# A hybrid decoder trunk: the weights of the attention steps combined a step earlier, and a beginning in quarters

## What is computed

```
proj = rms_norm(h) @ w_in                      # 1024 -> 2048: u (512), q, k, v (512 each)
y_pool = windowed means of u, 2/4/8/16 wide, minus u, times a 128x128 matrix per group
for each of 4 heads:                           # halves of 64 of q and k
    a = softmax(q1 k1^T / 8 + bias) - lam * softmax(q2 k2^T / 8 + bias)
    o = rms_norm(a @ v, subln_w) * 0.8
h = h + concat(y_pool, o) @ w_out
```

## Time and profile before

| what | value |
|---|---|
| time, median of 3 runs | 1526.26 us (1521.80 to 1531.88) |
| the profiled execution's own time | 1525.67 us |
| its span, first to last instruction | 1523.7 us |
| PE busy | 1415.4 us, 93% of the span |
| DVE, ACT, POOL busy | 695.0, 507.1, 395.0 us |
| mean granted clock of PE | 0.981 |

### The profile page before, as it was taken

One profiled execution on the slowest core, in us unless ns is written; L12 is line 12 of the kernel. 1 busy time (PEld: TensorE's weight loads), 2 busy tenths in 40 slices (PEclk: granted clock), 3 DMA queues, 4 the chain that ended last, 5 costly groups with the idle time before them and its releaser, 6 DMA issues.

```text
span 1523.7 us, 28397 instructions
## 1 busy us (share of the span) xinstructions
PE 1415.4 (93%) x11848; PEld 1185.4 (78%) x11848; DVE 695.0 (46%) x962; ACT 507.1 (33%) x723; POOL 395.0 (26%) x490
## 2 busy tenths in 40 slices
PE   6998889999999999898988989889789999999996
PEld 5766478888888888677777877777678888888885
DVE  5445533333333332766567576665533333333222
ACT  5233434232323222424424334244233232323221
POOL 2003412122212011534435343343322122212010
PEclk9998999999999999899999999999999999999999
DMA  7364612423233312002110220120032222233211
GB/s 268 146 197 164 201 54 86 164 83 110 83 120 115 113 67 83 28 29 70 42 56 29 68 72 28 56 68 30 1 136 100 104 89 99 94 120 114 100 53 56
DMA packets 31325, 140.92 MB, mean 92 GB/s; under 512 B 4457, under 2 KB 6761, under 8 KB 18954
## 3 DMA queue, kind: packets, MB, share of 16 engines
q1 hardware_dynamic: 31242, 139.75, 26.4%
HBM read 128.63 MB, written 11.11 MB: 92 GB/s over the span
## 4 chain that ended last, share of the span: by engine, by line
PE 83%; DVE 11%; issue 3%; ACT 2%; DMA 0%; POOL 0%; DVEq 0%; SPq 0%; ACTq 0%; POOLq 0%
PE P L1522 57%; PE P L1881 8%; PE P L1872 7%; DVE arena L1308 2%; PE P L1887 2%; DVE wl L1030 1%; PE P L1849 1%; DVE arena L1349 1%; DVE arena L1452 1%; PE P L2036 1%; PE P L2028 1%; PE P L1935 1%; ACT wh L695 1%; DVE arena L1396 1%; PE P L1722 1%
## 5 line engine op out<-in xcount | busy, mean ns | idle before, releaser
L1522 PE MATMUL P<-zh,wh 128*128 128x260 f16 x1728 | 334.4, 275 | 17.1 <-DVE wl L1030 13.2
L1522 PE MATMUL P<-zl,wh 128*128 128x260 f16 x1728 | 334.2, 275 | 0.0
L1522 PE MATMUL P<-zh,wl 128*128 128x260 f16 x1728 | 333.8, 274 | 0.0
L1522 PE MATMUL P<-arena,wh 128*128 128x260 f16 x1920 | 291.9, 273 | 5.3 <-DVE arena L1160 3.2
L1030 DVE SCALAR_TENSOR_TENSOR wl<-stage,wh 128x2048 f16<-128x2048 f32 (+1 forms) x77 | 189.4, 2460 | 224.5 <-ACT wh L661 196.0
L1522 PEld LDWEIGHTS P<-arena,wh 128*128 128x128 f16 x1920 | 185.6, 97 | 35.5 <-DVE arena L1160 3.3
L1522 PEld LDWEIGHTS P<-zh,wh 128*128 128x128 f16 x1728 | 166.7, 97 | 49.8 <-issue 23.0
L1522 PEld LDWEIGHTS P<-zh,wl 128*128 128x128 f16 x1728 | 168.0, 97 | 27.0
L1522 PEld LDWEIGHTS P<-zl,wh 128*128 128x128 f16 x1728 | 167.9, 97 | 27.0
L1522 PE MATMUL P<-arena,wl 128*128 128x260 f16 x960 | 184.5, 273 | 0.0
L1881 PE MATMUL P<-arena 128*128 128x128 f32 x1152 | 156.1, 288 | 28.8 <-issue 18.2
(11 more groups left out here) (300 smaller groups left out, 1583.6 us busy)
## 6 DMA issues: line engine op xcount, KB each, us to landing
stage<-w_gu SPq DMA_DIRECT2D x44, 1024.0 KB, 4.9
stage<-w_in SPq DMA_DIRECT2D x24, 1024.0 KB, 5.2
stage<-w_dn SPq DMA_DIRECT2D x16, 1408.0 KB, 5.8
arena<-cache_k SPq DMA_DIRECT2D x32, 256.0 KB, 3.5
stage<-w_out SPq DMA_DIRECT2D x8, 1024.0 KB, 6.5
arena<-cache_v SPq DMA_DIRECT2D x32, 256.0 KB, 2.9
arena<-delta_state SPq DMA_DIRECT2D x8, 512.0 KB, 3.6
o_ds<-arena SPq DMA_DIRECT2D x8, 512.0 KB, 6.7
```

The lines of the kernel that those rows point to most:

```text
L1522: mm = nc.tensor.matmul(pm[j][:, c, :], w[:, wslot, o:o + 128], x[:, k, c * CH:(c + 1) * CH], start=(k == first and w is wh and x is xh), ...
```

## The change

Loop, DVE: `combine` runs one step ahead. `combine(0)` stands between the leaving of tiles 4 and 5, and step s does maximum s+1, the leaving of its tile, `combine(s+1)`, and the weight split after that. Loop, PE: scores of step 1 stand ahead of the value transposes, whose copies are awaited only before the first turn; `decode_probs` stands before the turn of step 9, the first value product in step 9; the others stay. ACT copies the decode weights out before the turned ones. The last pooling group's split moves from behind the loop into step 15.

End: the first 12 matmuls of tile 0 of the output projection, then the last head's norm and the decode norm, then the rest of both tiles' pooling groups, then the heads. ACT takes the last head out before it turns to the decode norm.

Beginning: `hT` and the first weight unit arrive in quarters in turn, and ACT, DVE and PE work by quarters; both tiles of unit 0 grow together, and the statistics come after them, then all four strips. PE first multiplies a constant tile by itself 14 times (`WARM`, f32, 128 columns, result unused). The table of the bias is awaited alone (`t_in`), pooling weights and state have a semaphore of their own (`e_in`) and a later place, and the first three cache loads are spread among the strips' DMAs.

```diff
+            for q in range(4):
+                sp.dma_start(hT[:, 2 * q:2 * q + 2, :], xT[:, 2 * q:2 * q + 2, :]).then_inc(xq_in[q], 16)
+                sp.dma_start(stage[:, 0, q * UQ:(q + 1) * UQ], w_in0[ORDER0[0]][:, q * UQ:(q + 1) * UQ]
...
+            for q in range(4):
+                act.wait_ge(xq_in[q], 16)
+                for k in range(2 * q, 2 * q + 2):
                     nc.scalar.activation(zh[:, k, :], hT[:, k, :], ACT.Copy, scale=par[:, NORM[0] + k:NORM[0] + k + 1]
                                          ).then_inc(z_hi, 1)
...
+                for k in ((0, 1), (2,), (), (3, 4, 5, 6, 7))[q]:
+                    square_x(k)
...
+            for i in range(WARM):
+                nc.tensor.matmul(P[:, 7, 0:128], onesD[:, :], onesD[:, :], start=True, stop=True)
+            for k in range(KD):
+                pe.wait_ge(z_lo, k + 1)
+                if k % 2 == 0:
+                    pe.wait_ge(*((w0_lo, k // 2 + 1) if k < 6 else (lo_ready, 1)))
+                for n in range(2):
+                    mm = product(n, 0, 128 * n, zh, zl, KD, 256, (k,))
...
             statistics(0)
-            product(1, 0, 128, zh, zl, KD, 256, range(6, KD)).then_inc(mm_done, 1)
-            strip(0)
-            strip(1)
-            unit("in0", 0, 1, zh, zl, between=last_strips)
+            for h in range(H0):
+                strip(h)
+            unit("in0", 0, 1, zh, zl, between=lambdas)
...
             leave_in(4)
+            combine(0)
             leave_in(5)
             for s in range(16):
                 if s < 15:
                     maximum(s + 1)
-                combine(s)
+                if s in TILE_AT:
+                    leave_in(TILE_AT[s])
+                if s < 15:
+                    combine(s + 1)
+                if s in TILE_AT and TILE_AT[s] >= 12:
+                    pool_ext(TILE_AT[s] - 12)
                 if s in SPLIT_AT:
                     split_in(SPLIT_AT[s])
...
+                if s == 9:
+                    decode_probs()
                 turn_weights(s)
...
-            pe.wait_ge(dec_o, 1)
-            mixed(1, GROUPS[:3])
-            decode_stat()
-            pe.wait_ge(m_lo, 4)
-            mixed(0, GROUPS[:3])
-            head_stats(3)
-            mixed(0, GROUPS[3:])
-            mixed(1, GROUPS[3:])
+            pe.wait_ge(m_lo, 4)
+            mixed(0, GROUPS[:2])
+            head_stats(3)
+            decode_stat()
+            mixed(0, GROUPS[2:])
+            pe.wait_ge(dec_o, 1)
+            mixed(1, GROUPS)
+            mixed(0, (4, 5, 6))
             mixed(1, (4, 5, 6))
-            mixed(0, (4, 5, 6))
```

More of the change, by code:

```diff
@@ L228, in hybrid_trunk @@
         scratch = nc.dram_tensor("bias_scratch", (4, 128 * SKEW), f32).ap()
-        x_in, x2_in, c_in = sem("x_in"), sem("x2_in"), sem("c_in")
+        x_in, t_in, c_in, e_in = sem("x_in"), sem("t_in"), sem("c_in"), sem("e_in")
+        warm = sem("warm")
+        xq_in = [sem(f"xq_in{i}") for i in range(4)]
+        w0_in, w0_hi, w0_lo = [sem(f"w0_in{i}") for i in range(3)], sem("w0_hi"), sem("w0_lo")
         kv_in = [sem(f"kv_in{i}") for i in range(NKV)]
@@ L791, in _ @@
                     nc.scalar.activation(td[:, 0:512], P[:, 2, :], ACT.Copy).then_inc(ad_done, 1)
+                if s == 9:
+                    act.wait_ge(ad_ps, 1)
+                    act.wait_ge(consts, 2)
+                    nc.scalar.activation(aD, P[:, 3, 128:160], ACT.Copy)
+                    for g in range(NPG):
+                        ins = nc.scalar.activation(
+                            apad_slots(g), P[:, 3, 32 * g:32 * g + 32].rearrange("p (b h) -> p b h", b=NDEC), ACT.Copy)
+                    ins.then_inc(ad_done, 1)
+                if s == 15:
+                    pool_hi(3)
                 act.wait_ge(at_ps, s + 1)
@@ L1221, in _ @@
             decode_scale()
-            pool_lo(3)
             dve.wait_ge(n_hi, 4)
@@ L1791, in _ @@
                 if s == 9:
-                    decode_probs()
-                if s == 10:
                     decode_values(0)
```

122 lines of the change are left out of this document (53 added, 69 removed).

## The result

The changed kernel takes 1519.45 us, the median of 14 runs (1511.24 to 1521.22); the kernel before, run beside it, 1526.87 (14 runs, 1521.80 to 1532.45). The ratio is 0.9936, 95% interval 0.9920 to 0.9952. The gain is real, but 7.4 us by the medians and 9.8 by the ratio where 21.3 were forecast, and the time lies above the stated range. The page's totals of PE and DVE say little; PE's 1415.4 us have become 1426.7 (the same matmuls, more of them at a low clock), and the mean granted clock went from 0.981 to 0.974.

A forecast was written before the change was run, and what follows sets the result against it. PE's waits in the first 207 us, nearly all on DVE working in the wrong order, were taken as the bound; 7.3 + 5.9 + 2.5 + 2.7 + 0 + 2.9 = 21.3 from 1525.67 gave 1504.4 us, range 1497.0 to 1513.0.

The forecast's parts named there:

- beginning: Start through unit 0, statistics and four strips: work by quarters ends them at 24.7 instead of 32.0, gaining 7.3 us.
- steps 0 to 7: Loop's first half: reordering removes PE's waits in steps 0 and 1 and turns 3 and 7; gain 5.9 us.
- steps 8 to 11: Middle of the loop: 2.5 us from steps 8 and 9 and 2.7 from steps 10 and 11.
- steps 12 to 15: Last loop steps: nothing counted; the last pooling product starts at 186.8 and ends at 188.7 as before.
- end: Output projection after the loop: reordered splits and norms finish at 204.0 instead of 206.9, gaining 2.9 us.
- ACT becomes the first bound: In the beginning: ACT's casts, splits and squares set the pace, its last quarter out at 14.3 to 14.4 us.
- the last lands at about 11.7 again: In the beginning: bytes are unchanged, so the last load arrives at about 11.7 us, as before.
- slower rival: Beginning: stop and go of quarters holds PE at 1.2 GHz; decides from 187 slow matmuls, up to 1537.2 us; chance 0.02.
- Steps 8 and 9: Loop: new 4 us wait for decode weights, ready 8.1 us after fill 12, replaces two waits; gain 2.5 us.
- Steps 10 and 11: Loop: the same reordering removes waits of 0.5, 1.5 and 0.7 us; gain 2.7 us, bounds 1.2 and 3.5.
- Steps 12 to 14: Loop: DMA waits of 2.4 us vanish but the `pool_lo` chain lies under them; gain 0, bounds 0 and 2.5.
- the loop keeps its waits: Rival: loop waits move to `decode_probs` and scores, loop gives 2 of 11.1 us, time 1513.5 us; chance 0.20.

The follow-up runs named there:

- e5: Changed kernel with ACT copying turned weights before the next exponential behind splits, and decode probabilities and first value product back behind step 9's fill; 1514.29 us, ratio 0.9906.
- e3: Changed kernel, but in steps behind a weight split ACT copies the turned weights out before taking the next exponentials; 1516.78 us, ratio 0.9928 to the kernel before.
- e16: Changed kernel with 12 products of tile 1 held behind the statistics, strip 0 ahead, strip 1 behind, two strips inside unit 1; 1517.93 us, ratio 0.9918.
- e18: Changed loop with the beginning of before, but statistics behind all 96 products and four strips behind them; 1524.23 us, ratio 0.9961 to the kernel before.
- e4: Changed kernel with decode probabilities back behind step 9's turn and fill, and first value product back in step 10; 1512.62 us, ratio 0.9918.
- e8: Changed kernel, but DVE makes the decode weights ahead of the split of step 8 instead of behind it; 1513.86 us, ratio 0.9897.
- e17: The beginning of e16 (12 products held back, strips apart) with the loop of e10; 1512.66 us, ratio 0.9881 to the kernel before.
- e10: Changed kernel with decode probabilities back behind step 9's fill and decode weights ahead of the split in step 8; 1513.88 us, ratio 0.9903.
- e2: Kernel before with the changed order of loop and end alone, beginning as before; 1521.29 us, ratio 0.9953 to the kernel before.
- e9: Changed kernel with 13 further constant products between the quarters' products and 20 warm-up matmuls instead of 14; 1517.60 us, ratio 0.9923.
- e15: Changed loop with the beginning of before, plus 40 constant products at the start where PE would wait; 1517.67 us, ratio 0.9913.
- e12: Changed kernel with the first weight unit in two DMAs instead of four; 1514.34 us, ratio 0.9907 to the kernel before.

## Why the prediction was wrong

The measured gain was 7.4 us by the medians, 9.8 by the ratio, the forecast 21.3. The prediction's steps, by the marks of the two profiled executions (sum 5.7, missing 15.6):

| step of the prediction | forecast | measured |
|---|---|---|
| beginning, to T1 | 7.3 | 1.65 |
| steps 0 to 7, to the end of fill 12 (127.3, now 119.25) | 5.9 | 6.4 |
| steps 8 to 11, to the turn of step 12 (165.81, now 158.14) | 5.2 | −0.4 |
| steps 12 to 15, to the last turn (188.49, now 182.21) | 0 | −1.4 |
| end, to T2 | 2.9 | 1.4 |
| behind the mixer | 0 | −2.0 |

**Beginning: the term that failed most, by 5.65.** It has three parts. First, the walk by quarters ended 2.0 late: statistics at 20.76 instead of 18.8. The walk has DVE's low parts of the weights, 2.29 / 4 a quarter, and its additions, but not its casts `zl`, and so "ACT becomes the first bound" was wrong. The casts take 1.43 a quarter, and DVE is the bound:

```profile
14.54 1.43 DVE L1049 SCALAR_TENSOR_TENSOR zl<-hT,par,zh 128x520 f16<-128x520 f32 x2 [0.25 <-ACT zh L709]
...
15.88 1.09 DVE L1057 SCALAR_TENSOR_TENSOR wl<-stage,wh 128x512 f16<-128x512 f32 x1
...
16.90 3.71 DVE L1062 TENSOR_TENSOR ssq<-ssq,arena 128x520 f32<-128x520 f32 x5
```

The forecast had DVE's last low part done at 15.1; the five additions began at 16.90. That "the last lands at about 11.7 again" was wrong too: the last quarter of `hT` was there at 13.77. But DVE waited only 0.25 for it. In e5 it was there by 13.18, DVE worked from 9.26 on almost without a pause, and the statistics still started at 20.84. It was late since the DMA engines, full in both kernels from 3 to 9 us, moved less in the changed one (before, 351 and 423 GB/s in the same two stretches; only from 9 to 12 us did they move more, 410 against 356):

```profile
3.00:6.00 3.00, 3.00 (x20) 3.00 (x20) 0.12 (x1) 0.89 (x2) 0.00 (x0) 1.00 0.97 255
6.00:9.00 3.00, 1.54 (x15) 1.29 (x14) 2.53 (x4) 2.42 (x5) 0.00 (x0) 1.00 1.00 316
```

Second, the strips and the wait for `rstd` took 1.45 more, strips 4.72 for 3.5. Third, the first tile took 2.07 more, and 0.15 went to lambda's product. Some 3.3 of the second and third are the clock's, as e3 shows, whose trace has no fall (strips 3.50, tile 5.47). I took the tile at the 5.47 of the earlier trace rows, a row at full speed, while the change itself put a light stretch ahead of it; e16 and e18 show that this decided. The prediction's slower rival was the right mechanism in the wrong place ("the stop and go of the quarters"), and its argument against it, that units 1 and 2 have no gaps, looked past the statistics and strips. Its point, 187 slow matmuls, was far off: of unit 1's matmuls some 18 were slow (28.1 to 32.3 us, at twice 0.114). The same paragraph misread the kernel before: its matmuls were at full speed not after some 40 but after 23 or so, at 18.2 us.

**Steps 0 to 7: right**, 6.4 for 5.9, bounds 3.5 and 7. The waits of turns 3 and 7 went as worked out. What it missed is small: by the order of the queues, DVE's split, now behind the combine, delays the next maximum, thus the exponentials, and ACT copies the turned weights after those. In step 3 the last value product waits 1.06 for it:

```profile
80.87 1.16 PE L1736 MATMUL P<-arena 128*128 128x128 f32 x8 [1.06 <-ACT arena L811]
```

**Steps 8 and 9: the mechanism right, its size off, and so the sum.** The forecast had DVE's decode weights ready 8.1 behind the fill's end; it was 9.0 (119.25 to 128.2), and PE waited 5.2 instead of 4:

```profile
119.25 0.70 DVE L1074 TENSOR_TENSOR arena<-P,rstd 128x520 f32<-128x520 f32 x1 [5.48 <-PE P L1531]
...
120.04 3.40 POOL L489 TENSOR_TENSOR arena<-arena 128x527 f32<-128x527 f32 x3 [82.97 <-DVE arena L1074]
120.06 1.19 DVE L1117 TENSOR_SCALAR stage<-stage,arena 128x256 f32<-128x256 f32 x1
...
121.29 1.24 DVE L1120 SCALAR_TENSOR_TENSOR arena<-stage,arena 128x256 f32<-128x256 f32 x1
...
122.44 1.02 DVE L1161 COPY arena<-arena 128x8 f32<-128x8 f32 x1
...
126.42 1.26 POOL L495 TENSOR_TENSOR arena<-arena 128x512 f32<-128x512 f32 x1
...
126.64 1.06 DVE L1153 TENSOR_TENSOR arena<-arena 128x1 f32<-128x1 f32 x1
```

The combine's scaling and sum took 0.41 and 0.48 in step 1, without POOL (60.89 and 61.34 us). Here each lasts about as long as one of POOL's three instructions of 1.13, and so does a copy of 8 columns. The combine ended 3.3 behind the fill, and the forecast had 3.4. What it missed is the copy and sum of `pool_ext`, 1.2 instead of 0.4, and the split, 2.64 instead of 2.29. The rule of the Trainium skill (SBUF — State Buffer, on the two sides of SBUF: an exclusive lock, the loser fully blocked) that the prediction weighed gives the combine well, and the trace agrees by these rows. It does not agree everywhere: the split, which reads two SBUF tensors, began at 123.64 beside a POOL instruction from 123.52 to 125.01 and was 0.35 longer, not held for all of it; and for the scaling and the copy, which read one tensor, it asks for a two-port mode, which no view shows.

Two costs came on top of the wait. Behind it the clock fell (130 to 140 us: 0.76), so that the probabilities took 2.34 instead of 1.03 and the half fill 4.54 instead of 3.92. I had taken 0.79 from the earlier trace rows for the half fill but the undisturbed 1.03 for the probabilities. So the second half fill ended 16.4 behind the end of fill 12, where it was 16.1 before: a loss of 0.3 for a gain of 2.5. e4 and e8 show what the place is worth, by moving one block of ten matmuls or five short DVE instructions: 6.0 and 2.4 us of T2 − T1 in one trace each, 2.7 and 6 us by the ratios, of which only e8's is clear of the noise.

**Steps 10 and 11: the wait was wrong.** The three waits of 2.7 went, as forecast, but 3.0 of new ones came in their place (two for ACT's copies of the turned weights, 0.3 and 1.7, one of 1.0 for `pool_lo`), and the stretch from the second half fill to the turn of step 12 took 22.5 where it took 22.4. The sum had looked at the waits that go, not at the ones under them. A second series of POOL instructions also met the combine of step 10 (1.25 and 1.30 for its two parts), which the sum held at nothing. **Steps 12 to 14** were to give nothing, since the wait for `pool_lo` stays; it did stay (3.0, at 173.42) and so did the one before the sum (2.0), but 1.4 went in the same steps, with the clock at 0.79 from 170 to 180 us; I put the one down to the other, and no run tested it.

**End**: 1.4 for 2.9, just under its lower bound of 1.5. The last group's low part, at 196.52 before, is made at 184.79, and nothing waits for the norms any more; the two waits of 0.9 and 0.7 stayed, as forecast. The first k-tiles and the norm behind them ran at the low clock (1.57 us for two matmuls of 512 columns at 188.26), which the sum had not.

**Behind the mixer** nothing was changed, and the span is 2.0 longer there. Over all traces this part is 1315.1 to 1320.2 with identical instructions. I count it as the clock's scatter, not as an effect of the change; whether it is fed by what happens before 200 us stays open.

Of the rivals, "the loop keeps its waits" (0.20) came nearest in number, 1513.5, and was right in one of its two places: the waits went to `decode_probs`; none went to the scores. That its number is nearer is in part luck, since it keeps the 7.3 of the beginning. Two kinds of error run through the sum: one engine's own work or the next wait in line left out (`zl`, ACT's copies, `pool_lo`), and terms worked out at the upper level of the clock though the change itself made the places ahead of them lighter.

What stays open: why one trace with the bare wait (e3, T1 32.37) has no fall behind it where thirteen others have one, how much of an earlier T1 the loop's clock takes back as a rule rather than by chance, and whether both cures of the decode weights are worth more than one.

## What to carry to other kernels

When work is moved so that PE starts earlier, look at what is left behind it in one piece: statistics, a wait for a factor and some small products in a row cost little by their own rows, but the full tile behind them can run at 1.2 GHz for the most part, as here in thirteen of fourteen traces. Keep some finished-input products back to lay between such pieces; here 12 matmuls held back, with the strips in pairs, were worth 1.4 to 2.9 us of T1 (e17 against e10, e16 against the changed kernel), and their loss cost 3.3 (e18 against e2). None of the three is clear of the noise in the time of the whole kernel. And a block that is moved ahead of another (decode weights and probabilities ahead of a turn) is to be judged by what its own input waits for on the other engine; where several chains of a loop are nearly as late as each other, don't add up the cures: two that gave 2.7 and 6 us apart by the ratio gave 5 together, with intervals of 4 to 5 us. Walk every engine's whole queue, not only the instructions that the change is about.

## What the runs showed of the hardware

- The granted clock fell to 0.50 though PE was busy 7.76 of the 8 us around its start (e9, 20 to 28 us), and did not fall in e15 and e16. 12 strip matmuls took 3.50 us at the upper level (e3) and up to 5.82 where the clock fell in them (e8).
- Quarters in alternating DMAs moved 255 and 316 GB/s where whole halves and units moved 351 and 423, at a share of 0.97 and 1.00 of the DMA engines' time: a full share is no full rate. Halves of the weights among the quarters (e12) moved 301 and 310, and the last quarter landed no sooner, so the length of the weights' rows does not account for it alone.
- SBUF accesses of DVE as small as 128x1 and 128x8 took 1.06 and 1.02 us beside POOL's instructions; DVE's own 2.29 for a split became 2.64.
- One kernel's time moves by 10 us with 0.01 of mean granted clock (changed kernel: 1511.24 at 0.982, 1521.22 at 0.972).
